# Four things moved in the second block's side work: the decay matrix, the latent weights' request, the queries' scores and a solve scratch

## The reference

```
h    = rmsnorm(x, norm_w)
proj = h @ w_in                       # keys, queries, values, z, b, a; latent; moba
qkv  = silu(causal_conv(q, k, v))     # 4 taps: the last on ScalarE, three on VectorE
q, k = l2norm(q) * 128**-0.5, l2norm(k)
gc   = cumsum(g)                      # decay, from a, A_log and dt_bias
decay = exp(where(t >= j, gc[t] - gc[j], -inf))
L    = strict_lower(beta * (k k^T) * decay)
sol  = solve(I + L, [k * beta * exp(gc), v * beta])
A_qk = (q k^T) * decay
o    = chunked recurrence over sol, A_qk, q*exp(gc), k*exp(gc_end - gc)
y    = concat(mla(...) * silu(gate), rmsnorm(o) * silu(z), moba(...) * silu(gate))
x    = x + y @ w_out
```

## Time and profile before

| | |
|---|---|
| median of 3 runs | 1312.7 us |
| the profiled execution | 1312.83 us, of which its span 1311.0 us |
| TensorE busy | 1288.7 us (98%) |
| VectorE busy | 1033.3 us (79%) |
| ScalarE busy | 726.5 us (55%) |
| granted TensorE clock, mean | 0.997 |

### The profile page before, as it was taken

The page is one execution under the profiler, slowest core; times in us unless marked ns, Lnnn a source line. Parts: engine busy times, 40 slices in busy tenths (PEclk is TensorE's granted clock), DMA queues, the critical chain, the costliest instruction groups (busy, mean ns, idle before and its releaser), DMA issues.

```text
span 1311.0 us, 26108 instructions
## 1 busy us (share of the span) xinstructions
PE 1288.7 (98%) x10692; PEld 1228.1 (94%) x10692; DVE 1033.3 (79%) x1715; ACT 726.5 (55%) x1084; POOL 50.2 (4%) x48
## 2 busy tenths in 40 slices
PE   8999999999999999999999999999999999999997
PEld 8899999999999999999999999999998999889996
DVE  7999998677876777999997778776777756777565
ACT  6554566556544555544657555544567546566364
POOL 0000000000000000100000000000000110001100
PEclk9999999999999999999999999999999999999999
DMA  8555554565565466655355556555554324343232
GB/s 297 193 193 193 161 161 163 192 214 187 203 205 204 145 209 217 219 168 193 120 202 175 192 180 229 194 201 204 174 181 164 99 71 148 117 159 114 82 101 77
DMA packets 109711, 226.23 MB, mean 173 GB/s; under 512 B 6260, under 2 KB 17780, under 8 KB 109592
## 3 DMA queue, kind: packets, MB, share of 16 engines
q1 hardware_dynamic: 104656, 218.91, 49.6%
q10 hardware_dynamic: 4936, 5.65, 1.3%
HBM read 223.49 MB, written 1.06 MB: 171 GB/s over the span
## 4 chain that ended last, share of the span: by engine, by line
PE 81%; DVE 11%; ACT 4%; issue 2%; DMA 1%; POOL 0%; SPq 0%; ACTq 0%; POOLq 0%; DVEq 0%
PE bank L536 29%; PE bank L545 15%; PE bank L558 11%; PE bank L510 8%; PE bank L566 6%; DVE wlo L1904 4%; PE bank L597 3%; PE bank L515 2%; PE bank L625 2%; PE bank L647 2%; DVE w L2113 2%; PE bank L604 2%; ACT whi L1265 1%; DMA ring<-in_w_in 1%; DVE w L2457 1%
## 5 line engine op out<-in xcount | busy, mean ns | idle before, releaser
L1904 DVE TENSOR_TENSOR wlo<-ring,whi 128x1024 fp32r<-128x1024 f32 (+3 forms) x428 | 498.2, 1190 | 156.6 <-ACT whi L1265 135.4
L1265 ACT ACTIVATE whi<-ring 128x1024 fp32r<-128x1024 f32 (+3 forms) x428 | 431.3, 1024 | 321.6 <-PE bank L536 192.3
L536 PE MATMUL bank<-hboth,whi 128*128 128x256 f32 x3648 | 449.7, 276 | 0.0
L536 PEld LDWEIGHTS bank<-hboth,whi 128*128 128x128 f32 x3648 | 428.0, 192 | 1.8 <-issue 0.3
L545 PE MATMUL bank<-hboth,wlo 128*128 128x256 f32 x1824 | 247.4, 277 | 0.0
L545 PEld LDWEIGHTS bank<-hboth,wlo 128*128 128x128 f32 x1824 | 223.3, 192 | 3.8 <-issue 3.2
L558 PE MATMUL bank<-whi,hboth 128*128 128x512 f32 (+2 forms) x448 | 98.8, 363 | 0.0
L2113 DVE SCALAR_TENSOR_TENSOR w<-w,par 128x256 f32<-128x256 f32 x240 | 98.0, 477 | 0.0
L510 PE MATMUL bank<-w 64*64 64x64 f32 (+6 forms) x1312 | 89.7, 247 | 6.0 <-ACT w L1619 4.3
L558 PEld LDWEIGHTS bank<-whi,hboth 128*128 128x128 f32 x448 | 80.3, 189 | 9.3 <-issue 0.9
L510 PEld LDWEIGHTS bank<-w 64*64 64x64 f32 (+3 forms) x1312 | 75.2, 150 | 14.0 <-ACT w L1619 4.7
(11 more groups left out here) (312 smaller groups left out, 1532.3 us busy)
## 6 DMA issues: line engine op xcount, KB each, us to landing
ring<-in_w_in SPq DMA_DIRECT2D x100, 1024.0 KB, 5.1
ring<-in_w_ffn_down SPq DMA_DIRECT2D x22, 1024.0 KB, 5.1
ring<-in_w_ffn_gate SPq DMA_DIRECT2D x20, 1024.0 KB, 5.2
ring<-in_w_ffn_up SPq DMA_DIRECT2D x20, 1024.0 KB, 5.1
ring<-in_w_merge SPq DMA_DIRECT2D x8, 1024.0 KB, 5.1
ring<-in_w_out SPq DMA_DIRECT2D x8, 1024.0 KB, 4.9
ring<-in_w_oc SPq DMA_DIRECT2D x4, 1024.0 KB, 5.0
ring<-in_w_od SPq DMA_DIRECT2D x4, 1024.0 KB, 5.0
```

What stands on the lines that cost most here:

```text
L536: done = e.matmul(o, wh[:, k, cols(u)], paired(s_[:, k0 + k, :]), stop=False, skip_group_check=True, start=opens and k == 0 and s_ is sh a ...
L1265: e.activation(part_of(whi, j), part_raw(j), ACT.Copy).then_inc(*up("hi.a"))
L1904: e.tensor_tensor(part_of(wlo, j), part_raw(j), part_of(whi, j), ALU.subtract).then_inc(*up("lo.v"))
```

## The change

`TWO_PLAN`: the decay matrix (`decay` step 3) goes from place 11 to 14; the keys' taps and Silu (`taps` step 0) from 12 to 11; the queries' scores (`others` step 1) from 32 to 36. `Mm` gets a place of its own over the first half of `zs`, which is written only behind the last `z` part, and its first copy no longer waits for the queries' scores. `later_rows` stands behind part 9 and no longer behind part 5. All of this holds for both layers.

```diff
-        "others": [26, 32, 39, 39, 51],
-        "decay": [8, 8, 10, 11],
-        "taps": [12, 18, 32],
+        "others": [26, 36, 39, 39, 51],
+        "decay": [8, 8, 10, 14],
+        "taps": [11, 18, 32],
@@
         T_, LTc, TTc, Mm = (by64(b) for b in (big[:, 20 * S:22 * S], big[:, 26 * S:28 * S], bufI[:, 0:512],
-                                              bufH[:, 0:512]))
+                                              big[:, 4 * S:6 * S]))
@@
                     if lv > 1:
                         e.wait_ge(*at("MT", l, lv - 1))
-                    else:
-                        e.wait_ge(*at("A", l, 1))
                     e.activation(Mm[r], by64(bank("M", l, lv))[r], ACT.Copy).then_inc(*up("delta.a"))
@@
-                        if name == "qc" and i == 1:
+                        if name == "m0" and i == 1:
                             later_rows(l)
```

## The result

The changed kernel takes 1319.72 us (median of 6 runs, 1319.45 to 1321.48) against 1312.63 us before (6 runs). The ratio is 1.0057, with a 95% interval of 1.0047 to 1.0067: slower by 0.6%. The forecast was 1316.7. The direction and the place were right, the size was not: +7.1 us where +4.0 stood, at the upper end of the range by the medians and a little over it by the ratio.

A forecast was written before the change was run, and what follows sets the result against it. TensorE, busy 1288.7 of 1311.0 us, was taken as the bound. To 1312.83 us came later sums (1.35 + 0.65), clock (1.55 + 1.55) and requests (0.4), minus 1.6 for the solve: 1316.7 us, range 1314.3 to 1319.

The forecast's parts named there:

- What bounds: Whole kernel: TensorE is busy 1288.7 of 1311.0 us, so time moves only if its idle time or clock moves.
- Taps ahead of the decay matrix: Second block, ahead of the keys' squares: one idle stretch of 4.45 us; sums start 1.35 and 0.65 us later.
- The clock: TensorE behind the longer idle stretch: 1.2 GHz in both layers, costing 1.55 us each, bounds 0 and 3.1.
- The sum: 1312.83 us plus 1.35 + 0.65 + 1.55 + 1.55 + 0.4 minus 1.6 gives 1316.7 us.
- Table loads: ScalarE, two more a layer for Exp and the queries' Silu: hidden, cost nothing; bounds 0 and 1.28 us a load.
- Weights requested later: ScalarE behind part 9: a request sticks out ahead of the queries' squares in layer 0, +0.4 us in all.
- Queries' scores: Moved later on TensorE and VectorE: the solve's update wait of 0.8 us goes, -1.6 us over both layers.

The follow-up runs named there:

- e1: The kernel before with only the order of the decay matrix (14) and the keys' taps (11) changed: 1322.41 us, ratio 1.0074.
- e6: The changed kernel with the decay matrix at place 12 instead of 14, directly behind the taps: 1315.10 us, ratio 1.0017.
- e5_fill_half: The changed kernel with 20 matmuls of ones ahead of TensorE's wait for the keys' squares: 1313.57 us, ratio 1.0010.
- e13: The changed kernel with the keys' sums at place 20, squares and wait at 16, and 16 matmuls of ones of 64 columns behind that wait: 1330.86 us.
- e14: The changed kernel with the keys' sums at place 20, squares and wait at 16, and 8 matmuls of ones of 128 columns behind that wait: 1322.40 us.
- e9: The changed kernel with 10 matmuls of ones ahead of TensorE's wait for the keys' squares: 1317.38 us, ratio 1.0035.
- e11: The changed kernel with the keys' sums at place 20, ScalarE's squares left at 16, and the decay matrix at 12: 1312.93 us, ratio 1.0000.
- e3: The kernel before with only the request of the latent weights moved behind part 9: 1311.33 us, ratio 0.9992.
- e2: The kernel before with only the queries' scores at place 36 and the solve's scratch of its own: 1311.83 us, ratio 0.9997.
- both harmless parts: The kernel before with the late queries' scores, the scratch and the late weight request, in its old order of decay matrix and taps: 1311.20 us, ratio 0.9990.

## Why the prediction was right and wrong

*What bounds.* Right: only TensorE's idle time and clock moved the time. Its waits at lines 1619 and 2649 went, at line 1718 they grew.

*Taps ahead of the decay matrix.* Right to a few hundredths: 4.88 against 4.86 us to the decay matrix, 11.49 against 11.5 to the first square, sums later by 0.63 and 1.34 against 0.65 and 1.35. e1 shows that the exchange carries the loss, e6 that the remainder of part 10 is the link. The idle time I gave was 4.45 us and it is 4.9: I let the scores start at part 7's modelled end, 1164.4, where they start some 0.35 us ahead of it, and gave the scores 1.8 us where, start to start, they take 1.7.

*The clock. This is the step that failed.* That the clock falls in both layers was right. Its price was mis-sized: I took 1.55 us a layer from the earlier trace rows, with 3.1 as the upper bound, and 0.50 "for some 3 us" behind each wait. The profile shows 7.7 and 8.3 us at 0.50 behind the waits, which cost 3.8 and 4.1 us, above the bound; by e5_fill_half against the medians it is 6.1 us for both layers, about 3 each. (The profiled execution is 1.8 us above the median, so its clock may have been low for longer than usual.) The row I took it from was a wait of half the length with matmuls of 128 columns behind it. That the matmuls behind the wait matter is shown by e13 against e14, and by the table above; that the longer wait adds to it is suggested by e9 and e6 and not borne out by e11 and e1.

*The sum.* What is missing in it is almost wholly this term: 3.1 foreseen, 6.1 by the runs. The other terms were to add up to 0.8 us, and the ledger has 0.8 for them, but that is luck: the request was taken 1.3 us too high, the solve and the scores 1.0 too low, and 0.27 is assigned to nothing.

*Table loads.* Right: nothing, all hidden, the queries' too.

*Weights requested later.* I had +0.4, for a longer wait for the queries' squares. That wait vanished instead (-0.45 a layer), since the shifted TensorE arrives later there: in e5_fill_half, where it is not shifted so far, the wait is back, 0.35 and 0.22 us. And e3 gives 1.1 us for this part alone on the old order.

*Queries' scores.* The solve's 0.8 us went, as forecast. I missed that TensorE, with 1.8 us less to do before place 34, arrives at the transposes of the latent keys before VectorE's rotation is done: 0.5 us a layer. So -0.6 us and not -1.6, and e2 alone gives -0.6.

## What to carry to other kernels

When two engines hand work back and forth, a step moved by a few places is moved past every link of the pipeline that stands there: look at which copies and remainders it now waits for, not only at its own length. Two short waits of a matmul engine can be cheaper than one long one, as the clock may fall only with the long one. The price of the fall depends on the work that follows, so it should not be read off a wait with another kind of matmul behind it. A few matmuls of no use ahead of the wait, just as long as the wait, show what the clock costs. And where the helper engines have little slack, moving a wait away from one place may only find the next.

## What the runs showed of the hardware

Idle times of 1.9 to 2.4 us were sometimes followed by 1.2 GHz and sometimes not: 2.41 us in layer 0 before (yes) and 2.41 us in layer 0 with the late scores alone (no), 1.93 us in layer 1 of that kernel (yes) and of the kernel before (no). With both harmless parts even waits of 1.64 and 1.15 us close together were, in layer 0, and the like waits in layer 1 and in e3 were not. Idle times of 2.5 us and more always were, in these profiles.

The clock did not always fall while TensorE was idle. It fell 2.5 us ahead of the end of the wait in layer 0 of the changed kernel (1000.3, with the sums at 1002.8) and 2.2 us behind it in e9 (1003.8, with the sums at 1001.6), where TensorE had been busy in between. The time at 1.2 GHz was 3.4, 6.8, 10.2 or 13.7 us in every layer where there was any. A difference of 3.4 us between two of these is worth 1.7 us when TensorE is busy all along, about as much as single executions of the changed kernel lie apart; whether that is what sets them apart is not shown, as only one was profiled.

In e13 TensorE was shown as fully busy with matmuls of 64 columns for 7 us behind its wait, and was granted 1.2 GHz to their end.
